# Layer 1's attention with five score buffers in place, wider steps, and the boundaries' squares in the buffer of the low parts

## What is computed

```
h = h + rms_norm(f(rms_norm(h, g_pre)), g_post)       # each sub-layer

def sink_attend(q, k, v, bias, valid, sinks):         # layer 1's f, per block of 128 queries
    s = einsum('bqngd,bknd->bngqk', q, k) * 64 ** -0.5 + bias
    s = where(valid, s, -inf)
    m = maximum(max(s), sink)
    p = exp(s - m)
    denom = sum(p) + exp(sink - m)
    return einsum('bngqk,bknd->bqngd', p / denom, v)
```

## Time and profile before

| | |
|---|---|
| median of three runs | 2626.55 us (2624.94 to 2626.66) |
| the profiled execution | 2624.26 us, span 2622.5 us, granted clock .983 |
| busy of the span | TensorE 95%, DVE 62%, ACT 44% |
| layer 1's attention | 1415 to 1812 us of the span |
| costliest groups | the projections' matmuls L438 (2895 us of overlapping matmuls), the down units L461, `w_lo` L421, `w_hi` L416 |

### The profile page before, as it was taken

How to read it: one execution, slowest core, us unless ns; L and a number is a source line. 1 busy time by engine, 2 the same in 40 slices (tenths; PEclk the granted TensorE clock), 3 DMA queues, 4 the chain that set the end, 5 groups by cost and what they waited for, 6 DMA issues and landing times. The chain is left out here.

```text
span 2622.5 us, 37815 instructions
## 1 busy us (share of the span) xinstructions
PE 2485.6 (95%) x15455; PEld 2177.1 (83%) x15455; DVE 1619.1 (62%) x2921; ACT 1147.4 (44%) x1810; POOL 0.2 (0%) x4
## 2 busy tenths in 40 slices
PE   7999999999999999999998899989999999999997
PEld 4777989887788889999997676767788889999996
DVE  5677566576666556666655755665666556655556
ACT  4655454453443333343334766663434334332333
POOL 0000000000000000000000000000000000000000
PEclk9999999999999999999999999999999999999998
DMA  4222223223433333322233332231343333332322
GB/s 156 65 73 73 81 84 106 89 91 103 142 113 105 108 99 105 121 93 86 89 95 99 98 97 67 89 100 52 106 139 97 97 96 96 114 113 81 92 86 96
DMA packets 93433, 255.18 MB, mean 97 GB/s; under 512 B 12499, under 2 KB 43708, under 8 KB 91324
## 3 DMA queue, kind: packets, MB, share of 16 engines
q1 hardware_dynamic: 63884, 202.43, 24.4%
q10 hardware_dynamic: 29376, 50.33, 5.8%
HBM read 225.92 MB, written 26.74 MB: 96 GB/s over the span
## 5 line engine op out<-in xcount | busy, mean ns | idle before, releaser
L438 PE MATMUL banks<-act_hi,w_lo 128*128 128x272 f32 (+1 forms) x2952 | 975.0, 330 | 16.8 <-DVE act_lo L2262 7.5
L438 PE MATMUL banks<-act_hi,w_hi 128*128 128x272 f32 (+1 forms) x2952 | 960.9, 326 | 0.0
L438 PE MATMUL banks<-act_lo,w_hi 128*128 128x272 f32 (+1 forms) x2952 | 959.3, 325 | 0.0
L416 ACT ACTIVATE w_hi<-w_raw 128x1024 fp32r<-128x1024 f32 x366 | 380.7, 1055 | 698.3 <-PE banks L461 490.9
L421 DVE TENSOR_TENSOR w_lo<-w_raw,w_hi 128x1024 fp32r<-128x1024 f32 x366 | 442.6, 1223 | 366.3 <-ACT w_hi L416 366.0
L438 PEld LDWEIGHTS banks<-act_hi,w_lo 128*128 128x128 f32 x2952 | 560.2, 190 | 75.2 <-issue 21.3
L438 PEld LDWEIGHTS banks<-act_lo,w_hi 128*128 128x128 f32 x2952 | 561.1, 190 | 43.0 <-issue 1.7
L438 PEld LDWEIGHTS banks<-act_hi,w_hi 128*128 128x128 f32 x2952 | 559.5, 190 | 43.6
L473 DVE TENSOR_TENSOR acc<-acc,banks 128x272 f32<-128x272 f32 (+1 forms) x624 | 315.0, 520 | 191.7 <-PE banks L461 188.2
L461 PE MATMUL banks<-h_hi,w_lo 128*128 128x272 f32 (+1 forms) x1056 | 348.1, 330 | 30.0 <-DVE acc L473 13.1
L461 PE MATMUL banks<-h_hi,w_hi 128*128 128x272 f32 (+1 forms) x1056 | 345.7, 327 | 0.0
(11 more groups left out here) (231 smaller groups left out, 2591.1 us busy)
## 6 DMA issues: line engine op xcount, KB each, us to landing
w_raw<-wall SPq DMA_DIRECT2D x366, 512.0 KB, 3.6
normed<-h_scratch ACTq DMA_DIRECT2D x20, 352.0 KB, 3.7
h_scratch<-acc ACTq DMA_DIRECT2D x3, 2176.0 KB, 7.6
h_scratch<-acc ACTq DMA_DIRECT2D x3, 2048.0 KB, 8.3
gstates<-state ACTq DMA_DIRECT2D x4, 1024.0 KB, 6.3
gla_s<-gstates ACTq DMA_DIRECT2D x4, 1024.0 KB, 6.6
bias<-bias_scratch ACTq DMA_DIRECT2D x28, 128.0 KB, 2.3
bias_scratch<-bias_rows ACTq DMA_DIRECT2D x8, 383.0 KB
```

The lines of the kernel that those rows point to most:

```text
L416: nc.scalar.activation(WH[:, b % RING], WR[:, b % RAW], ACT.Copy).then_inc(w_hi, 1)
L438: last = nc.tensor.matmul(PS[:, bank, 0:n], w, a[X][:, k, o:o + n], start=(k == 0 and first), stop=(k == KT - 1 and w is wh and a is AH))
```

## The change

It has four parts.

1. *One buffer in place.* `probs` (3 buffers) and `scores` (2) become one `scores` of 5; the exponential and the scaling write where they read. The sink, which was copied in 2 of 4 items, is copied for each of the 64.
2. *Wider steps.* `exps` moves to step g+1, `divided` to g+2, `scaled` to g+3, `transposed` and `turned` to g+4, `values` to g+5, `hi` and `lo` to g+6 of a pair's second item. Windows are counted from s-1. On TensorE `values` stands ahead of the down units of its step, not behind them; on ACT the order in a step is `hi`, `exps`, `scaled`, `turned`.
3. *Uneven down units*, `UNITS`: 1, 3, 2, 2 at w=4 to 7 for half 0 and 2, 5, 4, 5 for half 1 (before: 2 and 4 each). The key and value blocks stand in three pieces at steps 18 to 20, `s_new` on TensorE at w=5 and on DVE at w=6 with a semaphore of its own (`xsw`), and the first block of the FFN in quarters.
4. *Squares in the low parts' buffer.* `SQ[X]` lies where `act_lo` lies, which is free at that time. The squares no longer wait for the first fold, the second norm's squares wait for half of the residuals each, the h loads wait for the earlier use of `act_lo` to be done, and the boundaries' operations stand at new steps.

```diff
@@ buffers
+        AL_AT = [at[0], at[0] + KT * WX[0] * 4]
         AL = [place(f"act_lo{X}", [P, KT, WX[X]], fp32r) for X in range(2)]
+        SQ = [place(f"squares{X}", [P, KT, WX[X]], offset=AL_AT[X]) for X in range(2)]
...
-        EX = place("probs", [P, 3, 2, NBW])
-        SS = place("scores", [P, 2, 2, NBW])
+        SE = place("scores", [P, 5, 2, NBW])
@@ act_square
-            if m:
-                act.wait_ge(ps_done, 2 * n - 1)
...
-                if m == 0:
-                    act.wait_ge(al_done, 2 * ACTS[prior])
             elif i:
-                act.wait_ge(ha_done, 4 * POSTS[i, X])
+                act.wait_ge(ha_done, 4 * POSTS[i, X] - 2 + 2 * m)
...
-            nc.scalar.activation(NM[X][:], ACC[X][:, part(m)], ACT.Square).then_inc(sq_done, 1)
+            nc.scalar.activation(SQ[X][:, part(m)], ACC[X][:, part(m)], ACT.Square).then_inc(sq_done, 1)
@@ act_h_load
             if y < 2:
-                act.wait_ge(ps_done, 2 * NORMS[i, "post", X])
+                act.wait_ge(al_done, 2 * ACTS[prior])
@@ act_step
-                if name == "Sq0" and i:
+                if name == "Sq1" and i:
                     act_h_store(act, i, X)
@@ tables
-        ACT_AT = {0: ("sq0",), 1: ("sq1",), 2: ("h0", "h1"), 3: ("root",), 5: ("h2",), 6: ("h3",), 8: ("Sq0",), 9: ("Sq1",),
-                  11: ("Root",), 12: ("hi0",), 14: ("hi1",),
-                  38: ("sq0",), 39: ("sq1",), 41: ("h0", "h1"), 47: ("root",), 50: ("h2",), 51: ("h3",), 52: ("Sq0",), 53: ("Sq1",),
-                  55: ("Root",), 57: ("hi0",), 60: ("hi1",)}
+        ACT_AT = {0: ("h0", "h1", "sq0"), 1: ("sq1",), 3: ("root",), 6: ("h2",), 7: ("h3", "Sq0"), 9: ("Sq1",),
+                  11: ("Root",), 13: ("hi0",), 16: ("hi1",), 39: ("h0", "h1", "sq0"), 41: ("sq1",), 44: ("root",),
+                  50: ("h2",), 51: ("h3", "Sq0"), 53: ("Sq1",), 58: ("Root",), 60: ("hi0",), 62: ("hi1",)}
...
+                  10: ("F1",), 12: ("n0a", "n0b"), 14: ("l0a", "l0b"), 15: ("n1a", "n1b"), 17: ("l1a", "l1b"), 40: ("f0",),
+                  42: ("f1",), 46: ("s0",), 48: ("s1",), 49: ("a0", "s2"), 50: ("a1", "s3"), 52: ("F0", "a2", "a3"),
+                  54: ("F1",), 59: ("n0a", "n0b"), 61: ("l0a", "l0b", "n1a", "n1b"), 63: ("l1a",), 64: ("l1b",)}
-        PE_AT = {3: "sum", 11: "Sum", 47: "sum", 55: "Sum"}
+        PE_AT = {3: "sum", 11: "Sum", 43: "sum", 57: "Sum"}
+        KV_AT = {18: (0, FIRST), 19: (0, SECOND), 20: (1, ALL)}
+        UNITS = ((0, 1, 4, 6, 8), (0, 2, 7, 11, 16))
@@ pe_att
-            for s in range(NIT + 4):
-                k, w = divmod(s, 8)
+            for s in range(NIT + 5):
+                k, w = divmod(s - 1, 8)
...
-                if 2 <= s < NIT + 2:
-                    transposed(s - 2)
+                if 4 <= s < NIT + 4:
+                    transposed(s - 4)
...
+                if w == 5 and 0 <= d < 4:
+                    s_new(d)
+                if 5 <= s < NIT + 5:
+                    values(s - 5)
                 if w >= 4 and 1 <= k < 8:
-                    units = len(down_units((k - 1) // 4)) // 4
-                    downs(k - 1, range((w - 4) * units, (w - 3) * units))
-                if d >= 0 and w == 4 and d < 4:
-                    s_new(d)
-                if 3 <= s < NIT + 3:
-                    values(s - 3)
+                    downs(k - 1, units_at(k - 1, w))
@@ biased
-                if i < 2:
-                    if g >= 2:
-                        dve.wait_ge(es, g - 1)
...
+                u, r, p = g % 5, g % 8, q % 8
+                if g >= 5:
+                    dve.wait_ge(tf, g - 4)
...
+                nc.vector.tensor_copy(SE[:, u, :, 2 * WIN:NBW], SINK[:, 2 * p:2 * p + 2].unsqueeze(2)).then_inc(sk, 1)
@@ dve_att
-                if 1 <= s <= NIT:
-                    divided(s - 1)
-                if s >= 4 and s % 2 == 1:
-                    lo(s - 4)
+                if s >= 7 and s % 2:
+                    lo(s - 6)
                 if s < NIT:
                     biased(s)
+                if 2 <= s < NIT + 2:
+                    divided(s - 2)
+                if w == 6 and 0 <= d < 4:
+                    s_new(d)
@@ act_att
-                if s >= 4 and s % 2 == 1:
-                    hi(s - 4)
+                if s >= 7 and s % 2:
+                    hi(s - 6)
                 if 1 <= s <= NIT:
-                    scaled(s - 1)
-                if s < NIT:
-                    exps(s)
-                if 2 <= s < NIT + 2:
-                    turned(s - 2)
+                    exps(s - 1)
+                if 3 <= s < NIT + 3:
+                    scaled(s - 3)
+                if 4 <= s < NIT + 4:
+                    turned(s - 4)
```

More of the change, by code:

```diff
@@ L352, in build @@
         tf, te, of, xh, xl = (sem("att_" + x) for x in ("pt", "pt_copied", "o", "hi", "lo"))
-        xsn, xsf, xsa, xsb, xex, xrc, xsc, xtf, xte, xof, xoh, xol = (
-            sem("samp_" + x) for x in ("scores_new", "scores", "biased", "masked", "exp", "rden", "scaled", "pt", "pt_copied", "o", "hi", "lo"))
+        xsn, xsf, xsw, xsa, xsb, xex, xrc, xsc, xtf, xte, xof, xoh, xol = (
+            sem("samp_" + x) for x in ("scores_new", "scores", "new_biased", "biased", "masked", "exp", "rden", "scaled", "pt", "pt_copied", "o", "hi", "lo"))
         def col(x):
@@ L1695, in downs @@
                         pe.wait_ge(q_ev, AQ[1, min(2 * k - 4, 7), 1])
+                    if k in (4, 6):
+                        pe.wait_ge(ms_done, NORMS[3, "post" if k == 4 else "pre", 0])
                 for m in units:
@@ L1814, in pe_att @@
                     pe.wait_ge(sa, NIT)
-                elif s == NIT + 2:
+                elif s == NIT + 4:
                     pe.wait_ge(te, NIT)
-                if s >= NIT:
-                    pe_first_block(pe, 2, "u" if w < 2 else "val", (FIRST, SECOND)[w % 2])
+                    pe_first_block(pe, 2, "val", ALL)
+                if NIT <= s < NIT + 4:
+                    pe_first_block(pe, 2, "u", range(2 * (s - NIT), 2 * (s - NIT) + 2))
             downs(7, range(len(down_units(1))))
@@ L1921, in dve_att @@
                         rest_after(dve, ("aq", q // 8, q % 8))
-                if k == 2 and w in (2, 4):
-                    rest_after(dve, ("kv", 1, w // 2 - 1))
-                elif w == 0 and k >= 2:
-                    for t in range(2):
-                        rest_after(dve, ("ao", (k - 2) // 4, (k - 2) % 4, t))
+                if s in (20, 21):
+                    rest_after(dve, ("kv", 1, s - 20))
+                if w < 2 and k >= 2:
+                    rest_after(dve, ("ao", (k - 2) // 4, (k - 2) % 4, w))
                 if w >= 4 and 1 <= k < 8:
-                    units = len(down_units((k - 1) // 4)) // 4
-                    adds(k - 1, range((w - 4) * units, (w - 3) * units))
+                    adds(k - 1, units_at(k - 1, w))
                 if d >= 0:
@@ L1977, in exps @@
                 X, q, i, blk, x0 = it_of(g)
-                u, r = g % 2, g % 8
+                r = g % 8
                 act.wait_ge(sa, g + 1)
-                act.wait_ge(sk, 2 * q + min(i, 1) + 1)
-                if g >= 3:
-                    act.wait_ge(tf, g - 2)
+                act.wait_ge(sk, g + 1)
                 for e in range(2):
-                    last = nc.scalar.activation(EX[:, g % 3, e, x0:], SS[:, u, e, x0:], ACT.Exp, bias=ST[:, r, 2 + e:3 + e],
+                    x = SE[:, g % 5, e, x0:]
+                    last = nc.scalar.activation(x, x, ACT.Exp, bias=ST[:, r, 2 + e:3 + e],
                                                 scale=-1.0, accum_out=ST[:, r, 4 + e:5 + e])
@@ L2078, in act_att @@
                         query(q)
[L2079 removed]
+                if w == 7 and k > 0:
                     downs_done(k - 1)
[L2081 to L2084 removed]
+                if s in (19, 20):
+                    keys_values(s - 19)
+                if s in (22, 23):
+                    by_token(s - 22)
                 if d >= 0:
```

98 lines of the change are left out of this document (45 added, 53 removed), and 4 rows, old and new, of the table DVE_AT.

## The result

The changed kernel takes 2632.85 us (median of 16 runs, 2626.59 to 2636.53) against 2625.78 us before (16 runs). The ratio is 1.0027, 95% interval 1.0018 to 1.0036: slower by .27%. The forecast was 2633 us. The time was met, but not by the sum as I wrote it: its terms were off and made up for each other, so that the total was luck, as the stages show.

A forecast was written before the change was run, and what follows sets the result against it. TensorE was taken to bound layer 1's attention, with 46.4 us idle. The terms -6.9 + 3.1 + 12.3 - .7 - 1.3 gave +6.5 us, so 2633 us against a median of 2626.55, range 2612 to 2646.

The forecast's parts named there:

- the four places of part 3: Steps 41, 45, 53 and 59 of layer 1's attention: TensorE waits of 4.9, 4.45, 4.3 and 4.25 us.
- Most signs: Turned copies' wait under 6 us, `lo` over 12, adds under 4, stage end 6 to 8 later, layer 1's FFN within 1.
- Part 3: Layer 1's attention from step 39 on: new waits of 31.65 us against 19.39 of idle time, net +12.3 us.
- the four long operations: ACT's or DVE's work directly ahead of a `hi` or `lo`, felt at steps 41, 45, 53, 59: 17.9 us together.
- the small waits of parts 2 and 3: Steps 18 to 38: mostly under 1 us at w=4, 6; later: `s_new` 4.1, `s_scores` 3.3, down units 3.35 us.
- The clock's term: TensorE's lower-clock stretches, seven expected instead of eight: -1.3 us, between -4 and +5.
- the third rival: Every long wait brings a lower-clock stretch, eleven or twelve instead of eight: 2639 to 2641 us, chance .13.
- Part 4's term: Second square no longer waits for the first fold, in the FFN stages and once in layer 0: -.7 us.
- in the ramp: Steps 0 to 17 of layer 1's attention: idle time of 14.15 us against 21.07, -6.9 us.
- in the middle: Steps 18 to 38 of layer 1's attention: waits of 9.05 us against 5.94, +3.1 us.

The follow-up runs named there:

- e2: Changed kernel with half 0's `root` at the end of ACT's step 43 instead of 44: 2628.90 us, 1.0010 of the kernel before.
- e4: Changed kernel with DVE's fold and two residuals of step 52 spread over steps 51 to 53: 2627.28 us, 1.0005 of the kernel before.
- e5: Changed kernel with `values` behind the down units of its step again: 2613.28 us, .9960 of the kernel before.
- e3: Changed kernel with the two first h loads behind `sq1` in ACT's step 41 instead of at step 39: 2632.16 us, 1.0025 of the kernel before.
- e1: Kernel before with only the squares moved to the low parts' buffer, with the waits that follow: 2617.39 us, .9972 of the kernel before.
- e11: Kernel before with `values` ahead of its step's down units, and DVE's `s_new` ahead of the adds: 2663.43 us, 1.0159 of the kernel before.
- e10: Changed kernel with `values` behind the units, the moves of e2, e3 and e4, `sq0` at step 38, next norm's chain spread: 2598.82 us, .9901 of the kernel before.
- e7: Changed kernel with the moves of e2, e3 and e4, next norm's chain later, `s_exps` at w=7 instead of w=6: 2629.75 us, 1.0029 of the kernel before.

## Why the prediction was right

**The mechanism was.** "Whatever ACT or DVE still has from the even step comes on top, uncovered": the four places of part 3 came within 1 us each, and e2 and e4 took two of them away with nothing in their place. Most signs came too: the wait for `lo` over 12 (25.7), the adds under 4 (2.3), four waits of about 4 us at the steps named. The turned copies' wait is under 6 only for the line that I had listed (4.1); with the other it is 9.4. The stage ends 8.8 us later instead of 6 to 8, and layer 1's FFN with what follows is 1.6 shorter instead of within 1.

**The weights were not.** Part 3 put 17.9 of its 31.65 us on the four long operations and named the place of `values` as what uncovers them. The runs show it the other way round in size: e5 leaves all four long waits (3.5, 4.5, 4.1 and 4.4 us, two of them now ahead of a unit) and is 17.8 us faster, while e2, e3 and e4 moved long operations for 4.0, .7 and 5.6. The term that stands for it in my sum, the small waits of parts 2 and 3, was not too small in idle time; idle time rose by 4.0 us and not by 8.5. What the sum left out is the lower clock (next paragraph). How much of e5's gain is clock is not shown: its profiled execution, the slowest of its five, has 41.0 us at the lower level too. In step 41 the price of the h loads was wrong as well: I set their 2.89 us behind `s_exps`, and most of them ran beside it (e3).

**The clock's term failed**: -1.3 forecast, and TensorE's busy time in the stage rose by 8.2 us. I counted eight stretches at the lower clock and expected seven; the trace of after has eleven, 41.0 us against 27.3, which is at most 6.8 us of loss more. Four of them stand at the four long waits (.50 to .58 above), the other seven behind waits of 1.6 to 3.1 us. The remaining 1.4 us of the 8.2 I can't place. The mechanism of the third rival, which I gave .13, is what happened, though its time (2639 to 2641) is not, since the idle time rose less than in my sum and the stages outside the attention came out shorter. The Trainium skill (TensorE: Matmul & The Clock Gate, "HAM oscillation — how this bites in real kernels") has the rule that gaps between bursts put the clock back each time. The trace agrees with it at all four long waits; by my estimate it would have added 6 us, right for this term, but 2639 for the time.

**Part 4's term was too small**: -.7 forecast, and e1 finds 8.2 us (3.7 to 11.3) for the part alone. I priced only ACT's two waits of .59 us in the FFN stages. They are gone, but half 0's squares in the attention had 7.7 us of waits on ACT, and in e1 these are gone as well, with 5.6 us of the stage. That the FFN stages gave 3.4 and 1.6 us is not shown. Up to the first score, the eleven profiles with the moved squares take 1411.77 to 1417.08 us, and the two without them, of the kernel before and of e11, 1415.17 and 1413.60; behind the attention e11, with the old squares, has the shortest rest of all:

```profile
1865.73:2661.60 795.87, 766.63 (x4730) 692.12 (x4729) 482.01 (x808) 289.42 (x391) 0.00 (x0) 0.99 0.32 102
```

**The idle time by stretches** came out near: cut at the scores of steps 17 and 39, it is 12.2 us in the ramp (14.15 forecast), 8.9 in the middle (9.05) and 29.7 from there on (31.65, and as a sign over 30). The table of stretches of the changed kernel, length less busy:

```profile
1411.82:1489.39 77.57, 65.34 (x350) 44.22 (x349) 56.56 (x152) 59.65 (x134) 0.00 (x0) 0.93 0.32 109
1489.39:1619.05 129.66, 120.72 (x777) 92.20 (x776) 69.54 (x196) 79.97 (x209) 0.00 (x0) 0.97 0.31 90
1619.05:1831.96 212.91, 183.22 (x1375) 148.46 (x1374) 121.17 (x329) 115.30 (x274) 0.00 (x0) 0.94 0.22 66
```


So +4.0 + 8.2 - 3.4 - 1.6 = +7.2 by these two profiles, where I had 8.5 - 1.3 - .7 = +6.5: a right total, by luck, from idle time too high, a clock's term with the wrong sign, and a gain of the squares too small. What stays open is how much the wide steps bring by themselves: e5 stands 10.7 us under the kernel before beside it and e1 8.2, and their intervals overlap; but e10, with the long operations moved too, stands 26.7 under it, 18.5 beyond e1. No run takes out the buffer in place or the uneven units singly.

## What to carry to other kernels

Where in-order engines finish short operations for one another, look at what work stands between the start of those operations and the instruction that waits for them. Here the place of the independent matmuls, ahead of that instruction or behind it, was worth 17.8 us, more than twice what the whole change cost. Place long operations of ACT and DVE where none of the short operations that TensorE waits for comes next in their queue (4.0 and 5.6 us for two of them); a table that was balanced for one order has to be balanced again for another. Count a wait of TensorE with what it does to the clock of the work behind it, not by its length alone. And before a few us of one profile are given a cause, look at the same stage in profiles of kernels that did not change there.

## What was not expected of the hardware

The busy time of the same 2497 matmuls goes roughly with the waiting around them: 357.45 us where TensorE is idle 29.5 (e10), 376.70 where it is idle 75.4 (e11), at granted clocks of .97 and .93, so .42 us of busy time to each us of waiting between these two ends. Single executions lie far from that line: with idle time of 46.9 and 47.5 us the kernel before is busy 361.1 us and e7 370.6, and e5, with less idle time than the kernel before, has .95 and 365.22.

The clock differs between executions of the same instructions, too. Up to the first score the changed kernel and e5 run the same code, and their profiled executions take 1411.82 and 1417.08 us, at granted clocks of .99 and .98. In one place, from 639 to 645 us, the kernel before shows .72; e11, with the same code there and the same wait of 3.1 us ahead of it, 1.00. That place in the kernel before and in e11, and the rows of e5, whose first answers to the first of the changed kernel above:

```profile
639.00:645.00 6.00, 5.17 (x16) 4.06 (x17) 5.11 (x8) 0.63 (x1) 0.00 (x0) 0.72 0.59 168
```

```profile
639.00:645.00 6.00, 5.22 (x22) 4.26 (x23) 5.83 (x9) 0.63 (x1) 0.00 (x0) 1.00 0.61 177
```

```profile
0.00:1417.08 1417.08, 1359.91 (x8230) 1206.75 (x8230) 890.87 (x1469) 599.61 (x802) 0.20 (x4) 0.98 0.31 99
1417.08:1820.26 403.18, 365.22 (x2497) 282.39 (x2497) 246.75 (x676) 254.93 (x617) 0.00 (x0) 0.95 0.27 85
```

That is why medians and stages are given side by side.
